# Silu rows made once and loaded by broadcast, and a fourth ring slot for modulation columns, in a two-block transformer kernel

## What is computed

```python
silu_c = jax.nn.silu(c)
silu_cc = jax.nn.silu(c_ctx)
for l in range(DEPTH):
    shift, scale, gate = jnp.split(silu_c @ w_mod[l] + b_mod[l], 3, axis=-1)
    shift_c, scale_c, gate_c = jnp.split(silu_cc @ w_mod[l] + b_mod[l], 3, axis=-1)
    n = rms_norm(h, pre_norm_g[l]) * (1.0 + scale[:, None]) + shift[:, None]
    ...
    h = h + gate[:, None] * rms_norm(y, post_norm_g[l])
```

## Time and profile before

| | us |
|---|---|
| median of 3 runs | 3014.25 |
| lowest and highest | 3010.16, 3015.16 |
| profiled execution, whole | 3005.49 |
| profiled execution, span of its instructions | 3003.7 |
| PE busy in the span | 2833.4 (94%) |
| DVE busy | 1947.7 (65%) |
| ACT busy | 1171.8 (39%) |
| POOL busy | 353.2 (12%) |
| DMA moved | 484.80 MB |

### The profile page before, as it was taken

One profiled execution on the slowest core, in us unless ns is written; L12 is line 12 of the kernel. 1 busy time (PEld: TensorE's weight loads), 2 busy tenths in 40 slices (PEclk: granted clock), 3 DMA queues, 4 the chain that ended last, 5 costly groups with the idle time before them and its releaser, 6 DMA issues. The chain is left out here.

```text
span 3003.7 us, 40478 instructions
## 1 busy us (share of the span) xinstructions
PE 2833.4 (94%) x15589; PEld 2347.8 (78%) x15589; DVE 1947.7 (65%) x3402; ACT 1171.8 (39%) x1874; POOL 353.2 (12%) x318
## 2 busy tenths in 40 slices
PE   5889999999899989999999989999899999999998
PEld 3567787878678867677877878755799999999886
DVE  4377787676868777443465568876866666666444
ACT  4343333333233354333343452333354444444443
POOL 5870000000000010000000005533300000000000
PEclk8999999999999989999999989965999999999999
DMA  9964264453526665232333544311345555555564
GB/s 366 355 206 151 88 203 152 129 165 107 157 88 224 224 223 188 95 119 95 123 120 105 177 135 156 122 62 38 129 143 171 178 191 178 188 180 186 193 194 151
DMA packets 154594, 484.80 MB, mean 161 GB/s; under 512 B 17169, under 2 KB 18193, under 8 KB 153233
## 3 DMA queue, kind: packets, MB, share of 16 engines
q1 hardware_dynamic: 107712, 381.21, 37.8%
q10 hardware_dynamic: 46688, 101.00, 10.4%
HBM read 469.03 MB, written 13.11 MB: 161 GB/s over the span
## 5 line engine op out<-in xcount | busy, mean ns | idle before, releaser
L1514 DVE TENSOR_TENSOR split_weights<-common,split_weights 128x1024 fp32r<-128x1024 f32 x644 | 798.5, 1248 | 623.6 <-ACT split_weights L2241 563.2
L2241 ACT ACTIVATE split_weights<-common 128x1024 fp32r<-128x1024 f32 x644 | 672.3, 1052 | 821.5 <-PE bank L1187 706.8
L1185 PE MATMUL bank<-split_weights,features 128*128 128x512 f32 x1920 | 802.9, 418 | 29.0 <-DVE split_weights L1514 12.1
L1187 PE MATMUL bank<-split_weights,features 128*128 128x512 f32 x1920 | 757.6, 395 | 0.0
L1186 PE MATMUL bank<-split_weights,features 128*128 128x512 f32 x1920 | 757.1, 394 | 0.0
L1185 PEld LDWEIGHTS bank<-split_weights,features 128*128 128x128 f32 x1920 | 366.0, 191 | 137.9 <-issue 49.9
L1187 PEld LDWEIGHTS bank<-split_weights,features 128*128 128x128 f32 x1920 | 365.1, 190 | 80.1
L1186 PEld LDWEIGHTS bank<-split_weights,features 128*128 128x128 f32 x1920 | 366.1, 191 | 77.9 <-issue 11.3
L1185 PE MATMUL bank<-ffn_input_split,split_weights 128*128 128x256 f32 (+1 forms) x1376 | 389.1, 283 | 0.8 <-issue 0.8
L1187 PE MATMUL bank<-ffn_input_split,split_weights 128*128 128x256 f32 (+1 forms) x1376 | 388.2, 282 | 0.0
L1186 PE MATMUL bank<-ffn_input_split,split_weights 128*128 128x256 f32 (+1 forms) x1376 | 387.8, 282 | 0.0
(11 more groups left out here) (299 smaller groups left out, 3323.6 us busy)
## 6 DMA issues: line engine op xcount, KB each, us to landing
common<-w_in SPq DMA_DIRECT2D x260, 512.0 KB, 3.3
common<-w_up SPq DMA_DIRECT2D x172, 512.0 KB, 4.3
first_block_work<-w_mod_cols ACTq DMA_DIRECT2D x256, 256.0 KB, 3.0
common<-w_out SPq DMA_DIRECT2D x104, 512.0 KB, 3.3
common<-w_down SPq DMA_DIRECT2D x84, 512.0 KB, 3.4
old_stream<-w_mod SPq DMA_DIRECT2D x64, 512.0 KB, 7.9
trig<-common ACTq DMA_DIRECT2D x32, 272.0 KB, 4.6
second_block_work<-trig SPq DMA_DIRECT2D x32, 272.0 KB, 2.8
```

The source lines that it names most:

```text
L1185: e.matmul(out_ap, xs[0], ws[0], start=first, stop=False)
L1187: return e.matmul(out_ap, xs[0], ws[1], start=False, stop=last)
L1514: e.tensor_tensor(lo, raw, hi.bitcast(F32), ALU.subtract).then_inc(*low_done.tick(("lo", m)))
L2241: e.activation(split_slots[:, 0, i, 0:words], raw_slots[:, m % RAW, 0:words], ACT.Copy).then_inc(*high_done.tick(("high", m)))
```

## The change

`silu_turn` is a new step ahead of the first stage. PE turns `silu_c` (128 x 16 for each of the two rows) into bank 5, DVE copies it to `scratch`, and ACT stores it in a DRAM tensor `silu_rows` of 2 x 2048 words. `silu_load` then reads a quarter of both rows from there, the same 4 KB for all 128 partitions, after the store has landed. The host's `c_rows` is gone, and so are `silu_tanh` and `silu_row` with their two slots, so that a row change takes two slots, none with DVE work. `MODRING` goes from 3 to 4, which moves each `mod_load` one tile further ahead of its piece. For the room of it `trig_w` moves to the region `common`, and the two tables that ACT makes (`trig_out`) lie in columns 1024 to 1295 of rows 0, 1 and 2, 3 of `hid`: a store has 256 runs of 1088 bytes then, not 128 of 2176. The first table waits for the last turn of x, which reads `hid`. DVE's first `mod_turn`, which writes `scratch`, waits for the store.

```diff
-MODRING = 3
+MODRING = 4
...
         self.do("steps")
+        self.do("silu_turn")
         self.first_stage()
...
                 self.do("silu_load", row, q, i)
                 yield
                 yield
-                for s in range(2):
-                    self.do("silu_tanh", row, s)
-                    yield
-                    self.do("silu_row", row, s)
...
-    trig_w = W.two(2, T2)
...
-    trig_out = [B.two(2, T2) for _ in range(2)]
+    trig_w = B.two(2, T2)
     assert B.at <= 5 * CH
+    trig_out = [hid[:, 2 * i:2 * i + 2, 2 * CH:2 * CH + T2] for i in range(2)]
...
+        def silu_turn():
+            tb = banks[5]
+            for s, n in seen.new(at("silu"), tb.claim("silu_turn")):
+                e.wait_ge(s, n)
+            for s_ in range(2):
+                done = e.transpose(tb[0:KT, s_ * P:(s_ + 1) * P], silu_c[:, :, s_], ident)
+            done.then_inc(*modulation_turned.tick(("silu_turned",)))
...
-            for s, n in seen.new(at("mod_done", c), at("mod_turned", before) if c else START):
+            for s, n in seen.new(at("mod_done", c), at("mod_turned", before) if c else at("silu_stored")):
...
+        def silu_turn():
+            for s, n in seen.new(at("silu_turned")):
+                e.wait_ge(s, n)
+            e.tensor_copy(scratch[0:KT, 0:2 * P], banks[5][0:KT, 0:2 * P]).then_inc(
+                *modulation_scaled.tick(("silu_kept",), ("free", "silu_turn")))
...
-            for s, n in seen.new(at("table_angles", j), at("table_stored", j - 2) if j > 1 else START):
+            for s, n in seen.new(at("table_angles", j), at("table_stored", j - 2) if j > 1 else at("x_turned", KT - 1)):
...
+        def silu_turn():
+            for s, n in seen.new(at("silu_kept")):
+                e.wait_ge(s, n)
+            e.dma_start(A["silu_rows"].rearrange("s (k p) -> k s p", p=P),
+                        scratch[0:KT, 0:2 * P].rearrange("k (s p) -> k s p", p=P)).then_inc(
+                *silu_stored.tick(("silu_stored",)))
...
         def silu_load(row, q, i):
-            for s, n in seen.new(at("mod_read", i - 1) if i else START):
-                e.wait_ge(s, n)
-            e.dma_start(silu_rows, A["c_rows"][q]).then_inc(*rows_loaded.tick(("c_row", row)))
+            for s, n in seen.new(at("silu_stored"), at("mod_read", i - 1) if i else START):
+                e.wait_ge(s, n)
+            e.dma_start(silu_rows, bc(A["silu_rows"][:, q * QUARTER:(q + 1) * QUARTER], 0, (P, 2, QUARTER))).then_inc(
+                *rows_loaded.tick(("silu_row", row)))
```

More of the change, by code:

```diff
@@ L1472, in down @@
                 done.then_inc(*products_done.tick(("used", m), *[("down", c)] * (f == FT - 1)))
-        tasks = dict(begin=begin, mod_products=mod_products, mod_turn=mod_turn, x_turn=x_turn, normed_turn=normed_turn,
+        tasks = dict(begin=begin, silu_turn=silu_turn, mod_products=mod_products, mod_turn=mod_turn, x_turn=x_turn, normed_turn=normed_turn,
                      mixed_turn=mixed_turn, products=products, turn_heads=turn_heads, scores_diff=scores_diff, scores=scores,
@@ L1619, in normed_first_split @@
                 *features_made.tick(*names))
-        def silu_row(row, stream):
-            words = silu_rows[:, stream, :]
-            for s, n in seen.new(at("silu_row_tanh", row, stream)):
+        def silu_turn():
+            for s, n in seen.new(at("silu_turned")):
                 e.wait_ge(s, n)
-            e.scalar_tensor_tensor(out=words, in0=mod_junk, scalar=1.0, in1=words, op0=ALU.add, op1=ALU.mult).then_inc(
-                *modulation_scaled.tick())
-            e.wait_ge(*modulation_scaled.last())
-            e.tensor_scalar(words, words, 0.5, None, ALU.mult).then_inc(*modulation_scaled.tick(("silu_row", row, stream)))
+            e.tensor_copy(scratch[0:KT, 0:2 * P], banks[5][0:KT, 0:2 * P]).then_inc(
+                *modulation_scaled.tick(("silu_kept",), ("free", "silu_turn")))
         def mod_piece(i, l, j, first, row, with_ctx):
-            for s, n in seen.new(at("mod_in", i), at("silu_row", row, 1)):
+            for s, n in seen.new(at("mod_in", i), at("silu_row", row)):
                 e.wait_ge(s, n)
@@ L2189, in vector_program @@
         tasks = dict(begin=begin, low=low, scale_rows=scale_rows, rows_scaled=rows_scaled, ssm_parameters=ssm_parameters, tables_end=tables_end,
-                     x_turn=x_turn, mod_turn=mod_turn, normed_first=normed_first, normed_first_split=normed_first_split, silu_row=silu_row, mod_piece=mod_piece, mod_scale=mod_scale, mod_gate=mod_gate,
+                     x_turn=x_turn, mod_turn=mod_turn, normed_first=normed_first, normed_first_split=normed_first_split, silu_turn=silu_turn, mod_piece=mod_piece, mod_scale=mod_scale, mod_gate=mod_gate,
                      normed_turn=normed_turn, normed_split=normed_split, mixed_turn=mixed_turn, bias_mask=bias_mask, lambda_sums=lambda_sums, lambda_made=lambda_made,
@@ L2279, in tables_end @@
                 e.wait_ge(s, n)
+        def silu_turn():
[4 more added lines that the diff above has]
+                *silu_stored.tick(("silu_stored",)))
         def silu_load(row, q, i):
-            for s, n in seen.new(at("mod_read", i - 1) if i else START):
+            for s, n in seen.new(at("silu_stored"), at("mod_read", i - 1) if i else START):
                 e.wait_ge(s, n)
-            e.dma_start(silu_rows, A["c_rows"][q]).then_inc(*rows_loaded.tick(("c_row", row)))
-        def silu_tanh(row, stream):
-            for s, n in seen.new(at("c_row", row), at("silu_row", row, 0) if stream else START):
-                e.wait_ge(s, n)
-            e.activation(mod_junk, silu_rows[:, stream, :], ACT.Tanh, scale=0.5).then_inc(
-                *tables_made.tick(("silu_row_tanh", row, stream)))
+            e.dma_start(silu_rows, bc(A["silu_rows"][:, q * QUARTER:(q + 1) * QUARTER], 0, (P, 2, QUARTER))).then_inc(
+                *rows_loaded.tick(("silu_row", row)))
         def mod_load(i, l, j, q):
@@ L2961, in lay_out @@
         "w_mod_cols": f["w_mod"].transpose(0, 2, 1).reshape(DEPTH, MOD_BLOCKS, P, 4, QUARTER).transpose(0, 1, 3, 2, 4),
-        "c_rows": np.broadcast_to(np.stack([f["c"][0], f["c_ctx"]]).reshape(2, 4, QUARTER).transpose(1, 0, 2)[:, None],
-                                  (4, P, 2, QUARTER)),
         "w_in": np.stack([moving(w, INC) for w in f["w_in"]]),
@@ L2987, in scratch_tensors @@
 def scratch_tensors(nc):
-    shapes = {"kept_stream": (P, LT, D), "trig": (SJ, P, 2, T2)}
+    shapes = {"kept_stream": (P, LT, D), "trig": (SJ, P, 2, T2), "silu_rows": (2, D)}
     return {n: nc.dram_tensor(n, shape, F32, kind="Internal").ap() for n, shape in shapes.items()}
```

6 lines of the change are left out of this document (3 added, 3 removed).

## The result

The changed kernel takes 3022.28 us (median of 8 runs, 3017.01 to 3025.61), the kernel before 3010.94 us (8 runs, 3009.28 to 3015.16): a ratio of 1.0035, 95% interval 1.0026 to 1.0044, so **11.3 us slower**. The forecast was no change, 3014.0. About 4.6 of them arise between 1850 and 1970 us, where the change alters nothing: the traces of five other kernels of this study lose the same there against that of before, those of the other seven at most 1.7 us.

A forecast was written before the change was run, and what follows sets the result against it. PE, busy 94%, was taken as the bound, with DVE bounding 200 to 250 us. Terms summed to -0.2 us, 3005.49 to 3005.3 in the profiled execution; with the median 8.8 us higher, 3014.0 us, range 3008.5 to 3020 (3004 to 3024 with rivals).

The forecast's parts named there:

- The table buffers: Table stores with twice the packets: +0.3 us, upper bound 16 us of DMA time; first table's wait already met.
- first row change: At 190 us: first piece runs in DVE's idle time, DVE's lead reaches PE, -3.4 us; bounds 0 and -5.3.
- Fifth row change: At 595 us: tanh goes, but two pieces stand between head rotations, +1.6 us; bounds -1.1 and +3.2.
- seventh row change: Some 15 us before the 1.63 us stall at 833.65: half that stall goes, -0.8 us; bounds -1.6 and 0.
- end of the attention: Layer 0, 896 us: a piece among the last gates delays DVE's copy, +1.6 us; bounds 0 and +3.2.
- the fourth slot: Fourth ring slot: costed at nothing; can remove only DVE's 5.0 us of tile waits, on which no PE idle ends.
- Head turns of the last group: At 781 and 834 us: the 12.50 us stall stays, last slot adds +0.5 us (bounds 0 and +2); seventh row change -0.8.
- the second rival: The broadcast load lands late: DVE waits at its head at row changes, +10 us, 3024; chance 0.13.
- The last pieces' end: Last piece stands 60 products earlier; old slots lie between 1150 and 1200 us where PE has no idle: nothing.
- The row changes pay everywhere: Faster rival: DVE's holes swallow the pieces at 595 and 896 us, -9.6 us, 3004.7; chance 0.27.
- The broadcast load lands late: Slower rival: silu rows land at 9 us, DVE waits 5.1 us at seven row changes, +10 us, 3024; chance 0.13.
- slower in other ways: Packets of the stores, or pieces at places held for harmless; no size given; chance 0.10.

The follow-up runs named there:

- after_ring3: Changed kernel with the ring of modulation columns at three slots again instead of four; 15.2 us slower than the kernel before.
- before_silu: Kernel before with the silu rows alone changed (20 slots fewer), ring of three and table buffers as before; 7.0 us slower than before.
- before_tables: Kernel before with only the table buffers moved (trig_w to common, trig_out to hid, first table behind the last turn of x); 11.4 us slower than before.
- after_plain_rows: Changed kernel whose row loads read the plain input rows per partition instead of the broadcast of turned rows; 8.5 us slower than the kernel before.
- silu_order_kept: Kernel before with the silu rows alone changed and two empty slots added at each row change, so pieces stay in place; 3000.27 us, 10.5 us faster than before.
- after_order_kept: Changed kernel with two empty slots more at each row change, so every piece stands where it stood before; 1.8 us faster than the kernel before.

## Why the prediction was wrong, step by step

Two steps failed, and neither alone is the whole loss.

**The table buffers.** The prediction costed their DMA packets (+0.3) and the first table's wait, and put trig_w's move at nothing without saying so. It looked for bounds at PE's waits for ACT and DVE, and took from POOL no row at all, though ACT waited 29.7 us for it. The move of the buffers costs 11.4 us in the kernel before, and 8.2 us in the one with the silu part: after_ring3 (15.2 slower) and before_silu (7.0) differ by it alone.

**The silu part.** Its terms, -3.4 + 1.6 + 0.5 - 0.8 + 1.6, come to -0.5 us; before_silu measures +7.0. By places, in the trace of the changed kernel against that of before: the first row change gave about 0 for -3.4, the fifth +3.1 for +1.6 (8.9 us behind at 580, 12.0 at 740), the seventh +2.5 for -0.8, the end of the attention +3.0 for +1.6. All four came out slower than their terms. With this 7.0, 11.4 for the buffers and -3.8 for the fourth slot the parts add up to 14.6 us against the 11.3 of the changed kernel, so they overlap.

**First row change, -3.4.** When the stall at 182 us begins, PE is 6.5 us behind (186.23 against 179.72 us), and 10.0 behind where that of 230 us ends: 3.5 us lost instead of 3.4 won. (The three stalls were 2.75 + 3.67 + 6.30 = 12.7 us and are 14.8.) But before_tables, with the silu rows of before, loses 3.9 us in the same stretch (5.6 to 9.5), so the silu part's own share is about 0. before_silu agrees: 2.4 us behind at the turn of 182 and 2.5 at that of 230. The step assumed that the rows land by 189.1 and that the first piece runs in DVE's idle time. In the changed kernel they were issued at 191.39 us and landed after 9.8 us, and the piece stands at the head of DVE's program, with the low parts behind it:

```profile
201.28 1.49 DVE L1639 CUSTOM_DVE_ANT_0 common<-first_block_work,common 128x512 f32<-128x512 f32 x1 [6.83 <-DMA first_block_work<-silu_rows]
```

The broadcast is not the whole of it: the plain rows of after_plain_rows took 8.8 us at this place, and DVE waits 5.88 us for them. Before, ACT waited for the landing and DVE did a low part meanwhile. The stall at 182 us comes ahead of the rows, and is 5.35 us in before_tables too: ACT waits for POOL ahead of the copy, 2.81 us in the changed kernel where it was 0.60. But in before_silu ACT waits 2.60 us there with the tables as before, and in silu_order_kept, whose program is the same up to there, 1.53; why is not known. With the order kept and the tables as before, PE goes from +1.9 us at 184.32 us to -2.9 at the turn of 230 and -1.8 at 273, a gain of 3.7 us: the ping-pong of ACT and DVE was worth what the term said, but not in the pieces' new places.

**Fifth row change, +1.6.** The stall went from 1.11 to 2.58 us, +1.5: right, by the mechanism named. It had a tail that the sum had not: the granted clock from 600 to 660 us is 0.97 where it was 1.00, and PE goes from 10.6 to 12.0 us behind. First before, then changed:

```profile
600.00:660.00 60.00, 58.09 (x262) 46.48 (x263) 50.35 (x117) 17.05 (x28) 0.00 (x0) 1.00 0.58 178
```

```profile
600.00:660.00 60.00, 55.50 (x247) 45.02 (x246) 53.23 (x122) 15.71 (x24) 0.00 (x0) 0.97 0.64 189
```

**Head turns of the last group.** The long stall is 12.51 us, 12.50 before: 0, within its bounds. The seventh row change was to give 0.8 us and took 2.5 (12.0 behind at 781, 14.5 at 834; the stall of 1.63 us at 834 is unchanged): the sign was wrong, because the rows landed late there, which was the second rival.

**End of attention, +1.6, bounds 0 and 3.2.** The two stalls went from 0.98 and 0.59 us to 1.59 and 1.90, +1.9; PE falls from 14.5 to 17.5 us behind across it. The mechanism held, the size was the upper bound.

**The fourth slot** was costed at nothing on the ground that no idle time of PE ended on the columns. That was so before; with the pieces moved and three slots DVE waits 5.42 us for a tile near 935 us, and PE falls from 18.3 to 20.3 us behind there, where the changed kernel stays at 17.5. The slot is worth 2 to 4 us. **The last pieces' end**, 60 products earlier, was put at nothing too. From 1046 to 1110 us the changed kernel gets 4.9 us back, but not by that: after_order_kept, with the pieces at their old places, gets 5.2 back there, and with three ring slots it is 1.5 (after_ring3) and 1.4 (before_silu). So most of it goes with the fourth slot, and 1.8 of it are lost again by 1200 us. The stated range, 3008.5 to 3020, does not follow from the bounds of the terms either: added up, the low ones give 3006 and the high ones 3024, without the 16 us of DMA time.

**The rivals.** "The row changes pay everywhere" gave -9.6 us; silu_order_kept, with its 10.5, is that rival's number, but it needs the slots that this change takes away; that the number is met is in part luck, since its stalls at 896 us did not go. "The broadcast load lands late" had the mechanism, and some 2 to 3 us of its 10. Neither they nor "slower in other ways", to which I gave 0.10, named POOL.

## What to carry to other kernels

Before a buffer is moved at no cost, look who reads and writes it and whether somebody waits for that engine: a wait of 29.7 us on the engine with 12% of the span told of a term of 8 to 11 us here, since it all lay in one stretch. When work is taken out of a schedule that counts in slots, keep its slots as empty ones and compare: here that was 13 and 17.5 us, and it turned a loss into a gain. A piece whose buffer is refilled from another engine's queue can cost what stands behind that refill, so look at its place before its length.

## What the runs showed of the hardware

The same subtraction of 128 x 544 on POOL took 1149 ns with one operand in another tile and 1358 to 1368 ns with both in one, at three spacings or starts; why is not known. A load that reads 4 KB and writes it to all 128 partitions landed in 5.2 to 6.0 us in median, by the kernel; one that reads a row of its own for each partition in 3.6 to 4.5 us. A store from 256 runs of 1088 bytes held ACT's queue 0.52 us at its issue, one from 128 runs of 2176 bytes 0.33.
